# Stationary operand of the second token half cut from 128 to 112 columns in the V stage of a PEER decoder layer

## The reference

```
g, idx = softmax of the 16 best (score, expert) of 8 heads, per token
h = x @ peer_u[idx]                    # one number per token and chosen expert
a = g * gelu(h)                        # exact gelu
out[token] = sum over chosen experts of a * peer_v[idx]
x <- LN(alpha*x + out)
```

## Time and profile before

| what | value |
|---|---|
| median of three executions | 2325.03 us |
| profiled execution, span from first to last instruction | 2323.1 us |
| what lies around the span, median minus span | 1.9 us |
| TensorE busy (matmul) | 2288.9 us, 99% of the span |
| TensorE's weight loads busy | 2081.4 us, 90% |
| VectorE, ScalarE, GpSimd busy | 1695.2, 1109.5, 596.5 us |
| V stage, first to last matmul start | 1612.3 to 2310.4 us |

### The profile page before, as it was taken

How to read it: one execution, slowest core, us unless ns; L and a number is a source line. 1 busy time by engine, 2 the same in 40 slices (tenths; PEclk the granted TensorE clock), 3 DMA queues, 4 the chain that set the end, 5 groups by cost and what they waited for, 6 DMA issues and landing times.

```text
span 2323.1 us, 45120 instructions
## 1 busy us (share of the span) xinstructions
PE 2288.9 (99%) x14858; PEld 2081.4 (90%) x14858; DVE 1695.2 (73%) x2702; ACT 1109.5 (48%) x1719; POOL 596.5 (26%) x420
## 2 busy tenths in 40 slices
PE   8999999999999999999999999999999999999997
PEld 8988899888898899999999999999888888888886
DVE  4444566655644577999999999997677766777657
ACT  4444555553343344554555455554444444444444
POOL 1000100000001027867656666566000000000000
PEclk9999999999999999999999999999999999999999
DMA  9788644566454656888888888888988887887874
GB/s 344 253 285 268 194 155 145 161 223 209 151 184 129 195 155 142 186 198 193 198 195 198 195 194 197 195 196 210 300 288 287 289 269 254 291 286 265 296 226 164
DMA packets 334141, 508.76 MB, mean 219 GB/s; under 512 B 69201, under 2 KB 216913, under 8 KB 326513
## 3 DMA queue, kind: packets, MB, share of 16 engines
q1 hardware_dynamic: 285856, 441.70, 62.5%
q0 software_dynamic: 47504, 65.31, 12.2%
q10 hardware_dynamic: 704, 0.75, 0.1%
HBM read 485.33 MB, written 21.23 MB: 218 GB/s over the span
## 4 chain that ended last, share of the span: by engine, by line
PE 97%; DVE 1%; DMA 1%; ACT 0%; issue 0%; POOL 0%; DVEq 0%; ACTq 0%; SPq 0%
PE ps L764 30%; PE ps L813 28%; PE ps L478 18%; PE ps L481 16%; PE ps L467 1%; PE ps L801 1%; PE ps L683 1%; PE ps L708 1%; DMA region<-in_peer_v_dram 0%; PE ps L514 0%; PE ps L745 0%; PE ps L600 0%; DMA region<-in_x_dram 0%; DVE y_out L1852 0%; PE ps L591 0%; DVE region L1583 0%
## 5 line engine op out<-in xcount | busy, mean ns | idle before, releaser
L1379 DVE TENSOR_TENSOR split_ring<-weight_ring,split_ring 128x1024 fp32r<-128x1024 f32 x288 | 351.4, 1228 | 310.7 <-ACT split_ring L886 299.0
L1310 POOL DMA_INDIRECT gates_scratch<-sb_gains x256 | 485.3, 1896 | 253.3 <-ACT sb_gains L1061 135.8
L813 PE MATMUL ps<-parts,temp_parts 128*128 128x512 f32 x2232 | 526.5, 389 | 1.1 <-ACT parts L1150 1.1
L764 PE MATMUL ps<-parts,u_hi 128*128 128x240 f32 x4096 | 498.8, 274 | 2.1 <-ACT u_hi L1066 2.1
L813 PEld LDWEIGHTS ps<-parts,temp_parts 128*128 128x128 f32 x2232 | 418.8, 188 | 88.6 <-ACT parts L1150 1.7
L764 PEld LDWEIGHTS ps<-parts,u_hi 128*128 128x128 f32 x4096 | 477.2, 190 | 2.3 <-issue 2.3
L886 ACT ACTIVATE split_ring<-weight_ring 128x1024 fp32r<-128x1024 f32 x288 | 302.9, 1058 | 339.2 <-PE ps L478 212.4
L478 PE MATMUL ps<-split_ring,parts 128*128 128x512 f32 x1872 | 429.8, 390 | 0.0
L1066 ACT ACTIVATE u_hi<-u_turned 128x1024 fp32r<-128x1024 f32 x256 | 271.7, 1062 | 326.0 <-DVE u_turned L1638 324.5
L478 PEld LDWEIGHTS ps<-split_ring,parts 128*128 128x128 f32 x1872 | 350.0, 188 | 72.7 <-issue 0.4
L1771 DVE TENSOR_TENSOR parts<-region,parts 128x512 fp32r<-128x512 f32 x372 | 245.4, 687 | 200.6 <-ACT parts L1150 200.6
(11 more groups left out here) (235 smaller groups left out, 1377.9 us busy)
## 6 DMA issues: line engine op xcount, KB each, us to landing
u_raw<-in_peer_u_dram SPq DMA_DIRECT2D x1024, 128.0 KB
region<-in_peer_v_dram SPq DMA_DIRECT2D x256, 512.0 KB, 4.8
weight_ring<-in_w_in_dram SPq DMA_DIRECT2D x96, 512.0 KB, 5.2
weight_ring<-in_w_mkv_dram SPq DMA_DIRECT2D x64, 512.0 KB, 4.0
gates_scratch<-temps POOLq DMA_DIRECT2D x16, 1024.0 KB, 7.2
weight_ring<-in_w_o_dram SPq DMA_DIRECT2D x32, 512.0 KB, 4.8
weight_ring<-in_w_mq_dram SPq DMA_DIRECT2D x32, 512.0 KB, 4.5
weight_ring<-in_w_mo_dram SPq DMA_DIRECT2D x32, 512.0 KB, 4.6
```

The costliest lines, as they stand in the source:

```text
L764: m = nc.tensor.matmul(ps[:, b, 0:ET], u[:, k * P:(k + 1) * P], x2T[n][kk][:, 0:ET], start=not done and kk == 0 and n == 0, stop=done and ...
L813: return nc.tensor.matmul(ps[:, 4 * t + q, :], e[:, t * P:(t + 1) * P], v[q], start=first and starts, stop=False, skip_group_check=True)
L1310: pool.indirect_dma_start(gates_by_one, bass.IndirectOffsetOnAxis(ap=idx_all[:, j:j + 1], axis=0), gate_all[:, j:j + 1], None, compute_op= ...
L1379: nc.vector.tensor_tensor(w_lo[j % SPLIT], raw[j % RAW], w_hi[j % SPLIT].bitcast(F32), ALU.subtract).then_inc(lo_ready, 1)
```

## The change

Matmuls of token half t = 1 in the V stage use the stationary columns 128 to 239 (112 of them) and write PSUM rows 0 to 111, instead of columns 128 to 255 and all 128 rows. Token half 0 is as before. The four matmuls of t = 1 that open a bank (block 0, first term) keep 128 columns, so that PSUM rows 112 to 127 are defined. Of the pads only that of `e_hi[0]` is still set to zero; the eight memsets of the held tiles are replaced by a plain semaphore increment. The number and the order of matmuls, loads, waits and DMAs stay as they were.

```
             def products(t, q, tiles_e, tiles_v):
-                c = slice(t * P, (t + 1) * P)
+                c = slice(t * P, min((t + 1) * P, ET))
                 hi, lo = tiles_v[0][q], tiles_v[1][q]
                 for n, (e, v) in enumerate(((tiles_e[0], hi), (tiles_e[0], lo), (tiles_e[1], hi))):
-                    m = nc.tensor.matmul(ps[:, 4 * t + q, :], e[:, c], v, start=False, stop=False,
+                    m = nc.tensor.matmul(ps[0:c.stop - c.start, 4 * t + q, :], e[:, c], v, start=False, stop=False,
                                          skip_group_check=True)
...
                 def part(t, q, e, v, starts):
 
-                    return nc.tensor.matmul(ps[:, 4 * t + q, :], e[:, t * P:(t + 1) * P], v[q], start=first and starts,
+                    opens = first and starts
+                    n = P if opens else min(P, ET - t * P)
+                    return nc.tensor.matmul(ps[0:n, 4 * t + q, :], e[:, t * P:t * P + n], v[q], start=opens,
                                             stop=False, skip_group_check=True)
...
             pool.wait_ge(u_used, UNITS - 1)
-            for e in e_hi + e_lo:
-                m = pool.memset(e[:, ET:T].bitcast(F32), 0.0)
-            m.then_inc(pad_set, 1)
+            pool.memset(e_hi[0][:, ET:T].bitcast(F32), 0.0).then_inc(pad_set, 1)
             pool.wait_ge(v_used, 4)
...
-            for held in held_e_hi + held_e_lo:
-                m = pool.memset(held[:, ET:T].bitcast(F32), 0.0)
-            m.then_inc(pad_set, 1)
+            pool.sem_inc(pad_set, 1)
             pool.wait_ge(e_lo_ready, NKEY - 32)
```

## The result

The changed kernel is slower. Six executions took 2334.01 to 2340.29 us, median 2336.64, against 2320.95 to 2325.95, median 2323.56, for six of the kernel before. The ratio on record is 1.0048, with a 95% interval of 1.0038 to 1.0058, 8.8 to 13.5 us; the two medians alone lie 13.1 us apart. The forecast was 2325.0 us, and even the upper end of the range, 2328, was passed. The traces of one execution each account for 10.4 us, as follows; the rest up to 13.1 us is within what the executions of one kernel differ by, 5.0 and 6.3 us.

The account below looks back on a forecast made before the run. TensorE's stream of load and matmul pairs was taken to bound the kernel, at 226.8 ns a V-stage pair. Every term was 0 us, leaving the median at 2325.0 us, with a range of 2317 to 2328 us.

Parts of the forecast that it names:

- The 13.2 ns: Part of each V-stage pair independent of moving columns; change taken as 0, bounds 0, 2.5 or 19.7 us saved.
- another slower outcome: Any other loss of 5 us and more, such as V-stage transfers starting worse; chance 0.03.
- Rival A and B: V-stage pairs: A, extra part shrinks with columns, -2.5 us, 0.26; B, stationary side counts, -4.7 to -20 us, 0.17.
- Rival C: V stage: 112 columns count as another geometry, each change draining TensorE; 188 us slower, about 2513 us; chance 0.04.
- over 228: Sign of the geometry rival: more than 228 ns a pair in the chain's piece of L813.
- The load is hidden: V stage: a 112-column load is 14 ns shorter but lies beside a 213.6 ns stream, so 0 us.
- The load in the U stage: L764's 111.7 ns a pair taken as the time a 128-column load needs; about 98 ns for 112.
- The pads, other waits, the tail: Fewer memsets worth 0, no wait added anywhere, 36 narrow matmuls at the end off the path.
- PSUM rows: V stage: writing 112 PSUM rows instead of 128 changes nothing, 0 us.

Follow-up runs that it names:

- e2: Changed kernel with 112 stationary columns in both token halves of the V stage, bank openers still 128: 229.0 ns a pair, 2330.2 us.
- e10: Kernel before, but half 1 reads 128 stationary columns from column 112 on (112 to 239): 230.1 ns a pair, 2333.11 us.
- e4: Changed kernel with all pads kept and the last two matmuls of each quarter swapped (half 0, 0, 1, 1, 1, 0): 233.4 ns, 2343.13 us, ratio 1.0082.
- e13: Changed kernel with half 1 reading 112 columns 144 to 255 instead of 128 to 239: 226.8 ns a pair; timed again, ratio 0.9999.
- e8: Kernel before with 112 stationary columns in the U stage, openers 128: 110.6 ns a pair instead of 111.7, 2317.17 us against 2325.59.
- e1: Changed kernel with its 112 columns, but all twelve memsets of the pads kept: 2334.18 us, ratio 1.0047.
- e14: Kernel before with both halves reading 128 stationary columns, 64 to 191: 226.8 ns a pair, 2323.99 us.
- e6: Changed kernel with 120 stationary columns in both halves: 233.4 ns a pair, 2344.62 us.
- e11: Both halves with 112 stationary columns and 480 moving columns instead of 512 in the V stage: 220.1 ns a pair.
- e12: Kernel before, 128 stationary columns, with 480 moving columns instead of 512 in the V stage: 216.9 ns a pair.
- e7: Changed kernel with 64 stationary columns in both halves: 230.1 ns a pair, 2334.82 us.
- e3: Changed kernel with 96 stationary columns in half 1 instead of 112, half 0 with 128: 232.3 ns a pair, 2339.21 us.
- e16: Kernel before with both halves reading 128 stationary columns, 32 to 159: 232.5 ns a pair, 2340.22 us.
- e15: Kernel before with both halves reading 128 stationary columns, 16 to 143: 233.4 ns a pair, 2342.80 us.

## Why the prediction was wrong

**The failed step** is the one headed "The 13.2 ns". It found rightly that a pair has 13.2 ns beyond the stream, and that the trace can't say what these hang on. It then bounded them on one side only (they stay, shrink or vanish) and took the change in them as 0. They grew, to 230.0 - 213.3 = 16.7 ns on average over the 2976 pairs at this line, wide ones included: 3.33 ns x 2976 = 9.9 us of the 10.2 us that the stage grew by. The rows that it leaned on, L478 and L813 agreeing to 0.1 ns "with quite different tiles", had one thing in common that I didn't see: all their stationary reads begin and end at multiples of 128 columns of their tiles. Agreement among such reads says nothing of others. The measured time falls among the outcomes that the prediction gave 0.03, "another slower outcome", for which it had no mechanism beyond the start of the V stage's transfers; that start moved by 0.4 us only.

**Rival A and B** had the wrong sign. **Rival C** had the right sign by luck, with the wrong mechanism: it priced changes of geometry, and it put the time at 2513 us. The prediction's sign for it, "over 228", came true at 230.1 ns all the same. e2 has no change of width and pays, e10 has no narrow operand and pays, e4 has half the changes and pays twice, e13 has all of them and pays nothing. The Trainium skill's rule, as the prediction quoted it from "TensorEngine Tiling (Array Packing)", by which 112 columns stay in the mode of 128, fits e13: going from 128 to 112 columns and back costs nothing there, at 226.8 ns a pair.

**The load is hidden**: right. It is 14 ns shorter, as estimated, and no matmul waited for its end. The Trainium skill ("TensorE: Matmul & The Clock Gate", section "Back-to-back issue gap") gives N/2.4 + 2.5 ns, 215.8 ns, and gives it for a matmul by itself, not for a pair with its load, as the prediction had read it. The traces have 226.7, 228.9, 230.0 or 233.3 ns for the same 512 columns; the position of the stationary read isn't in the rule.

**The load in the U stage**: not borne out. The prediction took 112 ns as the load's own time and 98 ns for 112 columns; e8 has about 110 ns, and what holds it there isn't known. It had no weight in the sum.

**The pads, other waits, the tail**: right. e1 shows the pads at zero. The 60 held matmuls on the path take 14.02 us against 14.08, though 12 of them are narrow.

**PSUM rows**: 0 was right; e13 writes the same 112 rows as the changed kernel at no cost.

**What is shown and what stays open.** Shown: the loss comes from which columns of the tile the stationary reads cover, it appears with 128 and with 112 columns alike when half 1's read ends at 239, and it is gone when it ends at 255. The contents don't explain it either. Half 1 of before and of e13 reads the 16 zeroed columns, which the changed kernel and e10 don't read; but e14 (64 to 191) and the held half 0 of before (0 to 127) read no zeroed column and have 226.7 ns, while e6 reads eight of them and has 233.3. Also shown: the loss depends on the order of the matmuls (e4 against e1) and on how many moving columns there are (e11 against e2, e12 against before), in averages most of which are shares of 6.67 ns. That fits two reads, the next load's and the running stream's, getting in each other's way depending on how their addresses lie, but the collision itself isn't in any record and is argued, not shown. Open is the rule for which reads are dear: e7's half 1 and e14 share an end and differ, so length or beginning count too.

## What to carry to other kernels

Cutting columns off a hidden load saved nothing here, and it cost 0.5%. Keep stationary reads at whole multiples of 128 columns of their tile, which was never dear beside 512 moving columns. If an operand has to be narrow, try the unused columns in front of the used ones: that was free for 112 of 128 columns in half 1 (e13), and no other width was tried that way. When a distance contains a part that no row explains, bound it on both sides, and ask of every row that "agrees" what all the rows have in common. Of the kernels here that do the whole layer's work none beat the one before, so the full 128 columns with zeroed pads stay the best.

## What the runs showed of the hardware

- The distance of a 512-column pair took few averages: 226.67, 228.9, 230.0, 232.2 (e3) and 233.3 ns, which is 0, 1/3, 1/2, 5/6 and 1 of a step of 6.67 ns, 16 cycles at 2.4 GHz, per pair. Over the six pairs of a quarter these are 0, 2, 3, 5 and 6 whole steps. e16, at 232.5, doesn't quite fit.
- The read position of the stationary operand alone moves the whole V stage by up to 19.3 us of 698.1 (e15: 717.4 us between first and last start). TensorE's waits at that line sum up to 0.3 us there.
- An effect of neighbouring operands shows in the wide matmuls too: in the changed kernel the places within a quarter range from 224.1 to 235.7 ns, two of them below the 226.7 of before.
